# A hybrid decoder layer on one core: the output weights split slice by slice under the last GLA output block, and the mixing norm's weight multiplied in before the rows are turned, with the first reads reordered

## What is computed

```python
hn = rms_norm(x, norm_mix)                 # x * rstd * weight
proj = hn @ w_in                           # 6160 columns: GLU, q, k, v, r, a_low, two branch gates
conv_out, ... = conformer_conv(u_glu, ...)
o, new_s      = gla_recurrence(q, k, v, log_a, gla_s, chunk)
gla_out = (rms_norm(o, gla_norm_g) * silu(r)) @ w_gla_out
h = x + (gc * conv_out + gg * gla_out) @ w_out
h = h + hier_moe(rms_norm(h, norm_ffn), ...)   # 32 experts, 2 per token
```

## Time and profile before

| | |
|---|---|
| median of 3 runs | 1838.77 us (1838.51 to 1839.80) |
| the profiled execution's own time | 1836.5 us |
| its span, first to last instruction | 1834.9 us |
| TensorE busy (share of the span), products | 1710.3 us (93%), 8996 |
| TensorE weight loads | 1494.0 us (81%) |
| VectorE busy | 1239.1 us (68%) |
| ScalarE busy | 913.8 us (50%) |
| GpSimd busy | 226.4 us (12%) |
| mean granted TensorE clock | 0.97 of full speed |
| chain that ended last | TensorE 80%, DMA 6%, weight loads 5%, VectorE 4%, ScalarE 2%, issue 2% |

### The profile page before, as it was taken

One profiled execution on the slowest core, in us unless ns is written; L12 is line 12 of the kernel. 1 busy time (PEld: TensorE's weight loads), 2 busy tenths in 40 slices (PEclk: granted clock), 3 DMA queues, 4 the chain that ended last, 5 costly groups with the idle time before them and its releaser, 6 DMA issues.

```text
span 1834.9 us, 24415 instructions
## 1 busy us (share of the span) xinstructions
PE 1710.3 (93%) x8996; PEld 1494.0 (81%) x8996; DVE 1239.1 (68%) x2000; ACT 913.8 (50%) x1085; POOL 226.4 (12%) x260
## 2 busy tenths in 40 slices
PE   6999989999899999989998996999999999999981
PEld 5999978777899999958997885788888888877771
DVE  5243789962566565653444556988989888888873
ACT  5262021114443333323433343787878877787763
POOL 3100111000000000001000123211111112221210
PEclk9999999999999999989999997999999999999995
DMA  4401222231124322153534327899999999999955
GB/s 172 139 36 59 70 93 100 88 107 38 65 87 137 123 86 86 43 197 98 183 120 161 104 88 264 321 360 376 364 384 383 383 392 388 377 375 376 359 204 194
DMA packets 101645, 366.18 MB, mean 200 GB/s; under 512 B 14389, under 2 KB 55569, under 8 KB 87744
## 3 DMA queue, kind: packets, MB, share of 16 engines
q1 hardware_dynamic: 78864, 308.06, 45.1%
q0 software_dynamic: 22704, 57.12, 9.7%
HBM read 324.35 MB, written 61.22 MB: 210 GB/s over the span
## 4 chain that ended last, share of the span: by engine, by line
PE 80%; DMA 6%; PEld 5%; DVE 4%; ACT 2%; issue 2%; DVEq 0%; PEldq 0%; SPq 0%; ACTq 0%; POOLq 0%
PE bank L999 77%; PEld bank L999 5%; DMA wraw_down<-in_w_expert_down 3%; PE bank L1401 2%; DMA wraw_gate<-in_w_expert_gate 1%; PE bank L1422 1%; DVE fbuf L2468 1%; DMA uo<-in_x_prompt 1%; DVE wL_gate L1889 0%; PE bank L1325 0%; PE bank L1204 0%; DMA stage<-xn_scr,kdT 0%; DMA h_scr<-ybuf,kdT 0%; DVE attn L2134 0%; DVE woL L1889 0%
## 5 line engine op out<-in xcount | busy, mean ns | idle before, releaser
L1889 DVE TENSOR_TENSOR wL_down<-wraw_down,wH_down 128x2048 fp32r<-128x2048 f32 x72 | 161.8, 2288 | 58.6 <-ACT wH_down L1490 58.6
L1889 DVE TENSOR_TENSOR wL_up<-wraw_up,wH_up 128x2048 fp32r<-128x2048 f32 x72 | 161.5, 2284 | 15.9 <-ACT wH_up L1490 15.9
L1889 DVE TENSOR_TENSOR wL_gate<-wraw_gate,wH_gate 128x2048 fp32r<-128x2048 f32 x72 | 161.6, 2286 | 6.3 <-ACT wH_gate L1490 6.1
L1490 ACT ACTIVATE wH_up<-wraw_up 128x2048 fp32r<-128x2048 f32 x72 | 134.1, 1910 | 59.2 <-DMA wraw_up<-in_w_expert_up 43.2
L1490 ACT ACTIVATE stage<-bank 128x512 f32<-128x512 f32 (+4 forms) x63 | 33.4, 546 | 255.3 <-PE bank L999 255.3
L2010 DVE SCALAR_TENSOR_TENSOR ybuf<-uo,gwork,ybuf 128x1024 f32<-128x1024 f32 x120 | 153.6, 1280 | 6.1 <-issue 6.1
L1490 ACT ACTIVATE wH_down<-wraw_down 128x2048 fp32r<-128x2048 f32 x72 | 133.8, 1910 | 12.8 <-DMA wraw_down<-in_w_expert_down 12.6
L999 PE MATMUL bank<-nTH,gateH 128*128 128x352 f32 x384 | 132.5, 345 | 5.3 <-DVE gateL L1889 5.3
L1490 ACT ACTIVATE wH_gate<-wraw_gate 128x2048 fp32r<-128x2048 f32 x72 | 134.2, 1923 | 2.6 <-DMA wraw_gate<-in_w_expert_gate 2.4
L999 PE MATMUL bank<-nTH,slabH 128*128 128x352 f32 x384 | 127.0, 331 | 5.9 <-DVE nTL L1889 5.6
L999 PE MATMUL bank<-nTL,slabH 128*128 128x352 f32 x384 | 124.9, 325 | 0.0
(11 more groups left out here) (309 smaller groups left out, 4297.2 us busy)
## 6 DMA issues: line engine op xcount, KB each, us to landing
wraw_gate<-in_w_expert_gate SPq DMA_DIRECT2D x36, 2048.0 KB, 14.9
wraw_up<-in_w_expert_up SPq DMA_DIRECT2D x36, 2048.0 KB
wraw_down<-in_w_expert_down SPq DMA_DIRECT2D x36, 2048.0 KB
slab_raw<-in_w_in SPq DMA_DIRECT2D x8, 2048.0 KB, 8.4
gate_scr<-stage POOLq DMA_DIRECT2D x16, 528.0 KB, 3.6
vr_scr<-stage POOLq DMA_DIRECT2D x32, 256.0 KB, 2.3
gate_raw<-in_w_in SPq DMA_DIRECT2D x16, 512.0 KB, 8.0
vrbuf<-vr_scr SPq DMA_DIRECT2D x16, 512.0 KB, 6.2
```

What stands on the lines that cost most here:

```text
L1490: return act.activation(out, in_, func, **kw)
L1889: return dve.tensor_tensor(out, x, y, op)
```

## The change

Two edits, both in. **Under the last block:** GLA block 7 runs its slices outside and its thirds inside, and counts each finished slice in a new semaphore `o_free` (the eighth after a drain). `woH` and `woL` take the stride of o, so slice k of w_out lies exactly over slice k of o, and slices 0 to 3 are loaded straight into their place in `woL` (`wo_in`) as each comes free; slices 4 to 7 are the four loaded early. ScalarE (whose `wo_high` now waits for `o_free` and for its load) and VectorE split the slices in K_ORDER; VectorE does five before mix(7) and three after. TensorE waits only for mix(6) and starts h tile 0 with slices 4, 5, 6, 0, 1, 2, 3, and 7 last. **In the head:** the norm weight is loaded as a row repeated on all partitions (`nmix`) and multiplied in with rstd in one instruction before the turn; `take_tile` and `nT_raw` are gone, and both halves of the split read the PSUM banks. The small parameter loads move to ScalarE's queue, ahead of its first work, and their turning behind that of tile 2; VectorE copies them out of bank 3 behind norm_tile(4). SP loads x0, nmix, x1, x2, 128 columns of the slab, x3, the other 384 columns, x4 to x8. ScalarE does one small Sqrt at once.

```diff
-        woH = at("woH", O_A, [P, KC, D], FR)
-        woL = at("woL", O_C, [P, KC, D], FR)
+        woH = at("woH", O_A, [P, KC, T], FR)
+        woL = at("woL", O_C, [P, KC, T], FR)
+        wo_in = at("wo_in", O_C, [P, KC, T])
@@ SP, head
             load_x(0)
...
+            sp.dma_start(nmix, a["norm_mix"].broadcast_to([P, D])).then_inc(norm_row_loaded, 16)
             load_x(1)
-            sp.dma_start(slab_raw[0][:, :, :], cols(SLABS[0])).then_inc(slab_loaded[0], 16)
-            for g in range(2, 5):
-                load_x(g)
+            load_x(2)
+            sp.dma_start(slab_raw[0][:, :, 0:P], cols(SLABS[0], P)).then_inc(slab_loaded[0], 16)
+            load_x(3)
+            sp.dma_start(slab_raw[0][:, :, P:], cols(SLABS[0] + P, 3 * P)).then_inc(rest_loaded, 16)
+            for t in range(4, NT):
+                load_x(t)
@@ SP, before h
+            sp.wait_ge(gw_free, NCH + KC - 1)
+            sp.dma_start(hh[0], x_tile(0)).then_inc(tile_loaded[0], 16)
+            for k in range(CC):
+                sp.wait_ge(o_free, CC + k + 1)
+                load_wo(k)
             sp.wait_ge(gw_free, NCH + KC)
-            sp.dma_start(hh[0], x_tile(0)).then_inc(tile_loaded[0], 16)
-            for k in range(4, KC):
-                sp.wait_ge(low_made, low(f"wo{k - 4}"))
-                load_wo(k)
             load_w(sp, W_GATE, 0, 0)
@@ TensorE, GLA blocks
+                    else:
                         for k in K_ORDER:
-                            last = gla_k(j, k, q)
+                            for q in range(3):
+                                last = gla_k(j, k, q)
+                            if k != CC - 1:
+                                last.then_inc(o_free, 1)
                 last.then_inc(gla_ready, 1)
+                if j == KC - 1:
+                    pe.drain().then_inc(o_free, 1)
-            pe.wait_ge(mixed, KC)
+            pe.wait_ge(mixed, KC - 1)
-            for k in range(KC):
+            for k in (*range(CC, KC - 1), *range(CC), KC - 1):
                 pe.wait_ge(low_made, max(low(f"wo{k}"), low(f"mix{k}")))
+            pe.wait_ge(mixed, KC)
@@ ScalarE, head
...
             act.wait_ge(const_step, 6)
+            f(rstd[0], eps_t, ACT.Sqrt)
-                act.wait_ge(nraw_made, t + 1)
-                f(nTH[:, :, t0], nT_raw[:, :, t0], ACT.Copy).then_inc(nTH_made, 1)
+                act.wait_ge(xT_ready, t + 1)
+                for q in range(2):
+                    last = f(nTH[:, 4 * q:4 * q + 4, t0],
+                             bk[4 + 2 * b + q].rearrange("p (k t) -> p k t", t=P)[:, :, 0:r], ACT.Copy)
             norm_high(0)
-            rms_tile(3)
+            slab_high(0, 0)
             norm_high(1)
-            slab_high(0, 0)
             norm_high(2)
-            for t in range(4, NT):
+            for t in range(3, NT):
                 rms_tile(t)
-                if t < 7:
-                    slab_high(0, t - 3)
+                if t < 6:
+                    slab_high(0, t - 2)
@@ ScalarE, before h
-            act.wait_ge(gw_free, NCH + KC)
-            for k in range(3):
+            for k in K_ORDER:
                 wo_high(k)
             mix_high(KC - 1)
-            for k in range(3, KC):
-                wo_high(k)
@@ VectorE, head
-                dve.tensor_scalar(xn[b][0:r, :], xt[t][0:r, :], rstd9[t][0:r, :], None, ALU.mult) \
+                if t == 0:
+                    dve.wait_ge(norm_row_loaded, 16)
+                dve.scalar_tensor_tensor(xn[b][0:r, :], xt[t][0:r, :], rstd9[t][0:r, :], nmix[0:r, :],
+                                         ALU.mult, ALU.mult).then_inc(xn_made, 1)
             norm_tile(0)
             norm_tile(1)
-            take_tile(0)
             norm_tile(2)
-            take_tile(1)
             norm_low(0)
-            norm_tile(3)
-            take_tile(2)
-            norm_low(1)
             slab_low(0, 0)
+            norm_low(1)
             norm_low(2)
+            norm_tile(3)
+            slab_low(0, 1)
+            norm_tile(4)
...
-            for part in range(1, 4):
+            for part in range(2, 4):
                 slab_low(0, part)
             for t in range(3, NT):
-                if t + 1 < NT:
-                    norm_tile(t + 1)
-                take_tile(t)
                 norm_low(t)
+                if t + 2 < NT:
+                    norm_tile(t + 2)
@@ VectorE, before h
-            wo_low(0)
+            for k in K_ORDER[:-3]:
+                wo_low(k)
             mix(KC - 1)
-            wo_low(1)
-            wo_low(2)
+            for k in K_ORDER[-3:]:
+                wo_low(k)
             mix_low(KC - 1)
-            for k in range(3, KC):
-                wo_low(k)
```

More of the change, by code:

```diff
@@ L227, in hybrid_layer @@
         wup = flat(ybuf)[0:RANK, D:D + QK]
+        nmix = onorm[:, :]
         prow = flat(kdn)[0:P, 0:P]
@@ L535, in hybrid_layer @@
         SPLIT_BASE = N_SLAB + 2 * NCH
+        K_ORDER = (*range(CC, KC), *range(CC))
         HIGHS = ([f"y{c}" for c in range(CC)] + [f"cw{j}" for j in range(KC)] + ["gl0"] +
@@ L539, in hybrid_layer @@
             HIGHS += ([f"gl{j + 1}"] if 1 <= j < KC - 1 else []) + ([f"mix{j - 1}"] if j else [])
-        HIGHS += ["wo0", "wo1", "wo2", f"mix{KC - 1}"] + [f"wo{k}" for k in range(3, KC)]
+        HIGHS += [f"wo{k}" for k in K_ORDER] + [f"mix{KC - 1}"]
         LOWS = ([f"y{c}" for c in range(CC)] + [f"cw{j}" for j in range(KC)] + ["gl0"] +
@@ L544, in hybrid_layer @@
             LOWS += ([f"gl{j + 1}"] if 1 <= j < KC - 1 else []) + ([f"mix{j - 1}"] if j else [])
-        LOWS += ["wo0", "wo1", "wo2", f"mix{KC - 1}"] + [f"wo{k}" for k in range(3, KC)]
+        LOWS += [f"wo{k}" for k in K_ORDER] + [f"mix{KC - 1}"]
         def high(part):
@@ L659, in load_wo @@
             def load_wo(k):
-                sp.dma_start(wo_raw[k % 4][:, :], a["w_out"][0][k * P:(k + 1) * P, :]).then_inc(wo_loaded[k % 4], 16)
+                dst = wo_raw[k % 4][:, :] if k >= CC else wo_in[:, k, 0:D]
+                sp.dma_start(dst, a["w_out"][0][k * P:(k + 1) * P, :]).then_inc(wo_loaded[k % 4], 16)
             sp.wait_ge(gw_free, NCH)
@@ L685, in _ @@
                 load_gl(j)
-            for k in range(4):
+            for k in range(CC, KC):
                 load_wo(k)
@@ L1357, in list_last @@
                 return last
-            mm(bk[7][:, 0:2 * NE], ones[0:1, 0:P], ident[0:1, 1:1 + 2 * NE], True, False, skip_group_check=True)
-            for k in range(KC):
+            for k in (*range(CC, KC - 1), *range(CC), KC - 1):
                 pe.wait_ge(low_made, max(low(f"wo{k}"), low(f"mix{k}")))
                 for hf in range(2):
-                    h_part(0, hf, k, k + 1).then_inc(h_ready, 1) if k == KC - 1 else h_part(0, hf, k, k + 1)
+                    last = h_part(0, hf, k, k + 1)
+                    if k == KC - 1:
+                        last.then_inc(h_ready, 1)
+            pe.wait_ge(mixed, KC)
+            mm(bk[7][:, 0:2 * NE], ones[0:1, 0:P], ident[0:1, 1:1 + 2 * NE], True, False, skip_group_check=True)
             for t in range(1, NT):
@@ L1504, in norm_high @@
                 t0 = slice(t * P, t * P + rows(t))
[L1505 to L1506 removed]
+                b, r = t % 2, rows(t)
+                act.wait_ge(xT_ready, t + 1)
+                for q in range(2):
+                    last = f(nTH[:, 4 * q:4 * q + 4, t0],
+                             bk[4 + 2 * b + q].rearrange("p (k t) -> p k t", t=P)[:, :, 0:r], ACT.Copy)
+                last.then_inc(nTH_made, 1)
             def slab_high(s, part):
@@ L1715, in wo_high @@
             def wo_high(k):
-                act.wait_ge(wo_loaded[k % 4], 16 * (k // 4 + 1))
-                split_high(f"wo{k}", woH[:, k, :], wo_raw[k % 4][:, :])
+                act.wait_ge(o_free, K_ORDER.index(k) + 1)
+                act.wait_ge(wo_loaded[k % 4], 16 if k >= CC else 32)
+                split_high(f"wo{k}", woH[:, k, 0:D], wo_raw[k % 4][:, :] if k >= CC else wo_in[:, k, 0:D])
             act.wait_ge(gw_free, NCH)
@@ L2218, in wo_low @@
             def wo_low(k):
-                split_low(f"wo{k}", woL[:, k, :], wo_raw[k % 4][:, :], woH[:, k, :])
+                split_low(f"wo{k}", woL[:, k, 0:D], wo_raw[k % 4][:, :] if k >= CC else wo_in[:, k, 0:D], woH[:, k, 0:D])
             dve.memset(attn[0:R, :, 0:R], 0.0)
```

78 lines of the change are left out of this document (37 added, 41 removed).

## The result

The changed kernel took 1825.97 us (median of four runs, 1825.37 to 1827.13), beside 1838.64 us for the kernel before (four runs, 1835.01 to 1839.80). The ratio is 0.9939, 95% interval 0.9927 to 0.9952: 11.2 us, between 8.8 and 13.4 (the two medians as they stand differ by 12.7). Forecast were 1825.7 us in a range of 1822 to 1832, so the time and the direction came out as said. The profiled execution took 1825.37 us (span 1823.7) against 1836.5 (1834.9): 11.1 us less, where 13.1 were forecast. Much of the closeness is thus luck: the old median lay 2 us above its profiled run, the new one 0.6. The profiled execution was forecast at 1823.4 and came 2.0 above that. The head gave 4.9 of 5.6 us; the last block and h tile 0 gave 7.5 as forecast, less 0.45 for something costed at nothing.

A forecast was written before the change was run, and what follows sets the result against it. TensorE, busy 93% of the span, was taken as the bound, with its waits and lower-clock time to win. Head 5.6 plus last block 7.5 made 13.1 us: profiled 1823.4, plus 2.3 to the median, 1825.7 us; range 1822 to 1832.

The forecast's parts named there:

- The head's chain: Start-up: loads, rms, norms, turns and PSUM passes put the first q product at 17.8 us, 5.6 us earlier.
- the repeated row's transfer: SP's queue in the head: nmix's 512 KB take 1.39 us behind x0, landing at 5.9, with x1 at 7.3.
- the 0.4 us allowed for gaps: End of the head: 0.4 us for gaps between instructions, from low 2's end at 17.4 to the first product at 17.8.
- the sign that was given for it: Start of the q stage: first q product at 17 to 18.5 us, with no pause to the stage's end.
- The half-rate stretch should move with the first product and cost the same.: Start of the q stage: products at half rate, 16 in 4.90 us, shift with the first product at unchanged cost.
- The slack behind: q stage: norm 5 done at 32.2, TensorE wants tile 5 at 33.7, so 1.5 us of slack remains.
- The last block: GLA block 7 and h tile 0: no TensorE idle stretch, upper clock kept, tile 0 ends 7.5 us earlier.
- the zeroing of bank 7: Behind h tile 0: two small products moved there cost nothing, since they stand before waits that end later.
- all durations: From h tile 1 to the end: every duration stays as before.
- Carried to the end: Whole span: a stage that starts earlier ends earlier by as much, so 5.6 and 7.5 add to 13.1 us.
- Rival C: Expert blocks: loads keep their own pace and the gain is given back, time 1836 to 1841; chance 0.04.
- rival D: Head: nmix lands near 23.8 us or later and norm 0 waits, kernel slower, 1844; chance 0.02.

The follow-up runs named there:

- Runs 6 and 7: On the changed kernel: 6 issues x tile 1 ahead of the norm weight's repeated row, 1825.75 us; 7 replaces that row's load by a GpSimd fill of ones, 1825.77 us.
- Run 9: The changed kernel with added products that nothing reads, put where TensorE idles in the head; 1822.76 us, ratio 0.9924 to the kernel before.
- Run 3: The changed kernel with TensorE's wait for mix(7) ahead of h tile 0 put back; 1831.19 us, ratio 0.9965 to the kernel before.
- run 4: The changed kernel with the loads of w_out slices 0 to 3 all issued when block 7 has ended; 1829.70 us, ratio 0.9959 to the kernel before.
- run 5: The changed kernel with VectorE's mix(7) ahead of the subtraction of slice 0 instead of behind it; one execution, 1824.12 us.
- run 1: The kernel before with the head's edits alone, last GLA block and h as before; 1834.06 us, ratio 0.9980.
- run 10: The changed kernel with x tile 1 ahead of the norm row, tile 2 in banks 2 and 3, added unread products, rms 6 to 8 later; 1821.81 us, ratio 0.9909.
- run 11: The changed kernel itself, measured again on the same chip; 1826.28 us, ratio 0.9936 to the kernel before.

## Why the prediction was right, point by point
**The head's chain.** Right in kind, 0.7 us off in size. ScalarE's seven issues took 3.0 us instead of 2.6, and rms 0 was ready at 6.9 instead of 6.6, which did not matter. The term that was mis-sized is the repeated row's transfer. It was put at 1.39 us behind x0, and landed 2.2 us behind it (6.71 after 4.47, forecast 5.9); x1 came another 1.6 behind the row, at 8.27 where 7.3 was forecast. Runs 6 and 7 confirm it: without the row in front x1 lands at 5.9. All later steps have the forecast lengths, one us later (tile 1's turns 11.4 for 10.2, tile 2's 14.1 for 13.0, high 2 16.1 for 14.9); and the 0.4 us allowed for gaps was not needed. The first q product, at 18.58, thus just missed the sign that was given for it (17 to 18.5). The table load took 1.28 us with the next instruction behind it, as in the earlier trace rows; so the price of 2.66 that the Trainium skill gives (ScalarE: Activation LUTs, What ACT_TABLE_LOAD costs) does not apply here, and rms 0 won 0.4 us in all.

**"The half-rate stretch should move with the first product and cost the same."** True of the two profiles compared (17 and 16 slow products), but not a law: it is 9 to 20 from run to run. The step should have stood in the range as 1.7 us.

**The slack behind.** 1.5 us forecast; norm 5 ended at 32.5 and TensorE came at 34.2, 1.7. Run 9 agrees from the other side: there TensorE came sooner, waited 0.85 us ahead of tile 5, and turned it 2.2 us before the change did.

**The last block.** Right step by step. Slice 0's load was issued at 965.82, 7.5 us into the block (forecast 7.4), and ScalarE copied it 3.6 us later (forecast 4.0). mix(7) ended 0.4 us earlier, counted from the block's start, than forecast, TensorE had no pause over 0.2 us within tile 0 after its first 0.48, and 7.50 us were saved up to the last product. Run 3 shows the split into idle and lower clock (3.8 and 2.3), run 4 the closeness of VectorE behind TensorE, run 5 that TensorE is the bound.

**The step that failed**, though small, is "the zeroing of bank 7 ... cost nothing: they stand before waits that end later". No wait ends later there: TensorE goes straight from tile 0 to tile 1 and pays 0.45 us. It was priced as hidden without naming what hides it. The forecast that from h tile 1 on "all durations" are as before missed by as much again: from the first product of tile 1 to the last of tile 8 it is 117.75 us before and 117.74 in run 1, but 118.2 in all eleven profiles with the edits around the last block. No run shows why.

**Carried to the end.** Both parts arrive, within what the stages between them vary by: the shift is 4.9 us at the first q product, 5.1 at the turns of tile 8, 4.7 at block 7, 11.7 at tile 1 of h, 10.6 at the first expert product, 11.2 at the end. From the first to the last gate product (high by high) of the expert blocks it took 633.3 us before and 633.6 after, and 632.1 to 635.4 over all thirteen profiles, with no order by kernel. Rival C (given back there) is thus refuted up to some 2 us, and rival D did not happen: the row landed at 6.7, and D needed 23.8.

## What to carry to other kernels
A region that a long product still reads can be handed over piece by piece: loop the pieces outside, count each one, and let loads and conversions follow; then look at what the first consumer waits for besides them, because one coarse wait (run 3) gives most of it back, with interest from the clock. In a start-up, look at what stands in the queue in front of the transfer that the longest chain waits for (here 512 KB cost it 2.4 us), and order the first reads by that chain. Where only a few us are at stake, compare places in the trace, not medians, and look between them for stretches at the lower clock before a shift is put down to an edit.

## What the runs showed of the hardware that was not expected
- Products that nothing reads raise the clock: with 23 of them among the turns (run 9), no q product ran at the lower level, nor in run 10, while in the eleven profiles without them 9 to 20 did each. The turns of tile 8 began 2.2 us sooner than in run 11. The median was 3.5 lower, but these two intervals overlap. They do not keep it up for sure: in run 10 it was at 0.50 from 11.1 to 14.4 us.
- The moment at which the clock rises after the first q product varied from 2.8 to 6.3 us between runs of nearly the same code, and the stretch at 0.50 near 90 us was absent, 3.4 or 6.8 us long.
- The profile's clock column can miss a low start. It said 1.00 throughout the slow q products of the kernel before and of the change, while the spacing was twice the later one; in runs 6 and 7 the same column showed 0.50 for the same spacing. In the head, read the spacing beside it. Run 6:
```profile
17.40:23.70 6.30, 6.21 (x21) 6.21 (x22) 5.60 (x9) 5.85 (x11) 5.20 (x12) 0.50 0.79 285
```
- The clock stayed at 1.00 over pauses of TensorE of 1.2 and 2.1 us (run 4), and fell in those of 4.3 (run 3) and 5.1 us (before, run 1). But near 88 us it fell behind a pause of only 1.2 us in twelve of the thirteen profiles.
- The same transfer lands at different times: x tile 3 of the old head was taken at 16.26 in one run and 17.41 in another, and the first q product moved by as much (23.46, 24.61).
